# Latent attention with keys on partitions and split products, first two stages fused, on a hybrid decoder layer

## The reference, cut to what matters

```python
xn = rms_norm(x, g_pre)
qa, ka, va, za, cq, ckv_raw, kpe_raw, zb, ma, mb = _split_in(xn @ w_in)
oa = _combine_groups(outs, lses)        # three dilated groups, merged by softmax weights
q = (rms_norm(cq, g_q) @ w_uq)          # 8 heads of 64 + 32 (rotary)
c_kv = rms_norm(ckv_raw, g_kv); k_pe = rope(kpe_raw)
k_nope = c_kv @ w_uk;  v = c_kv @ w_uv  # 64 wide, per head
s = (q_nope . k_nope + q_pe . k_pe) * MLA_SCALE      # 2048 x 2048, causal
ob = softmax(s) @ v
pa = (oa * silu(za)) @ w_proj_a;  pb = (ob * silu(zb)) @ w_proj_b
y = x + rms_norm((sigmoid(ma) * pa + sigmoid(mb) * pb) @ w_out, g_post)
```

## Time and profile before

| | |
|---|---|
| median of 3 executions | 4331.28 us (4324.72 to 4336.58) |
| profiled execution, its span | 4348.47 us, 4346.9 us |
| busy in the span: PE, DVE, ACT, POOL | 3522.2, 1369.5, 951.2, 373.6 us |
| norm and latent stages | 0 to 194.4 us of the span |
| dilated stage | 194.4 to 1536 us |
| gates | 1536 to 2094.8 us |
| latent attention | 2094.8 to 2866 us |
| samples (both stages) | 2866 to 3750 us |
| join | 3750 to 3919 us |
| projection, output | 3919 to 4346.9 us |

### The profile page before, as it was taken

How to read it: one execution, slowest core, us unless ns; L and a number is a source line. 1 busy time by engine, 2 the same in 40 slices (tenths; PEclk the granted TensorE clock), 3 DMA queues, 4 the chain that set the end, 5 groups by cost and what they waited for, 6 DMA issues and landing times. The chain is left out here.

```text
span 4346.9 us, 56892 instructions
## 1 busy us (share of the span) xinstructions
PE 3522.2 (81%) x19368; PEld 2973.9 (68%) x19368; DVE 1369.5 (32%) x3898; ACT 951.2 (22%) x1842; POOL 373.6 (9%) x490
## 2 busy tenths in 40 slices
PE   4899999999999999999799999934444465417989
PEld 3777777777777789999577767723334465317967
DVE  4112222222322321000355556512221222484333
ACT  4322222222222211111244344410000111001021
POOL 0000000000000000000000000002322333002300
PEclk6999999999999889999899999965555777558999
DMA  3243333222333122211200000035552222465543
GB/s 106 89 147 106 106 105 102 88 84 83 95 105 122 56 68 73 74 67 55 66 12 12 14 11 12 10 101 188 185 177 80 61 53 63 141 227 184 175 127 121
DMA packets 310894, 407.39 MB, mean 94 GB/s; under 512 B 72793, under 2 KB 270138, under 8 KB 305290
## 3 DMA queue, kind: packets, MB, share of 16 engines
q1 hardware_dynamic: 278154, 249.11, 19.0%
q0 software_dynamic: 23312, 151.28, 10.0%
q10 hardware_dynamic: 9216, 4.20, 0.3%
HBM read 317.28 MB, written 175.28 MB: 113 GB/s over the span
## 5 line engine op out<-in xcount | busy, mean ns | idle before, releaser
L109 PE MATMUL dil_J<-all_xT_hi,dil_w_hi 128*128 128x512 f32 x1152 | 475.0, 412 | 18.5 <-DVE dil_w_lo L695 17.7
L111 PE MATMUL dil_J<-all_xT_hi,dil_w_lo 128*128 128x512 f32 x1152 | 455.8, 396 | 0.0
L110 PE MATMUL dil_J<-all_xT_lo,dil_w_hi 128*128 128x512 f32 x1152 | 455.5, 395 | 0.0
L109 PE MATMUL gate_ps<-all_xT_hi,gate_w_hi 128*128 128x416 f32 x960 | 338.8, 353 | 9.1 <-DVE gate_w_lo L950 9.1
L110 PE MATMUL gate_ps<-all_xT_lo,gate_w_hi 128*128 128x416 f32 x960 | 337.3, 351 | 0.0
L111 PE MATMUL gate_ps<-all_xT_hi,gate_w_lo 128*128 128x416 f32 x960 | 337.1, 351 | 0.0
L1232 PE MATMUL mla_S<-mla_k,mla_q 96*128 96x512 f32 (+3 forms) x640 | 281.8, 557 | 15.4 <-ACT mla_p L1119 8.7
L720 DVE CUSTOM_DVE_ANT_0 dil_sm<-dil_S,dil_bias 128x256 f32<-128x256 f32 (+1 forms) x384 | 125.0, 363 | 501.2 <-PE dil_S L812 428.7
L109 PEld LDWEIGHTS dil_J<-all_xT_hi,dil_w_hi 128*128 128x128 f32 x1152 | 218.4, 190 | 72.5 <-DVE dil_w_lo L695 17.8
L1260 PE MATMUL mla_O<-mla_v,mla_pT 128*128 128x66 f32 x2176 | 264.8, 271 | 2.6 <-DVE mla_pT L1179 1.7
L666 ACT ACTIVATE dil_sm<-dil_sm,dil_neg 128x256 f32<-128x256 f32 (+1 forms) x384 | 156.6, 455 | 486.6 <-DVE dil_neg L726 486.6
(11 more groups left out here) (264 smaller groups left out, 6102.9 us busy)
## 6 DMA issues: line engine op xcount, KB each, us to landing
out_win_sample<-in_state_win POOLq DMA_DIRECT2D x8, 8128.0 KB, 27.0
sdil_kv<-in_state_win SPq DMA_DIRECT2D x72, 512.0 KB
scr_gates<-gate_out POOLq DMA_DIRECT2D x24, 1040.0 KB, 4.6
sdil_qb<-scr_hs SPq DMA_DIRECT2D x32, 768.0 KB
dil_raw<-in_w_in SPq DMA_DIRECT2D x36, 512.0 KB, 4.1
proj_gm<-scr_gates SPq DMA_DIRECT2D x40, 416.0 KB, 3.3
out_win_sample<-in_state_win POOLq DMA_DIRECT2D x8, 1984.0 KB, 11.5
scr_oa<-dil_rec SPq DMA_DIRECT2D x192, 66.0 KB, 1.6
```

Of the source, the lines that this page charges most:

```text
L109: pe.matmul(out, w[0], x[0], start=first, stop=False)
L110: pe.matmul(out, w[0], x[1], start=False, stop=False)
L111: return pe.matmul(out, w[1], x[0], start=False, stop=last)
```

## The change

**First stages.** stage_norm and stage_latents become stage_front, one pipeline of 22 slots: slot i turns tile i, projects tile i-2 and turns the latents of tile i-4. The weights are loaded by POOL's queue from the start. The copy of the projection to SBUF (L327) is dropped, g_q is applied as a row, the latents' transposes leave in 2 copies instead of 4, and cqT, ckvT, kpeT are stored after every fourth tile.

**Latent attention.** Keys lie on partitions: a unit is now a tile of 128 keys by up to 512 queries, 40 units ("ticks") per head. A first product (A, one fp32r matmul) gives scores with queries on partitions, only to take row maxima; they are put as row 96 of the high queries, so that the transposed scores S come out with the maximum subtracted. S and the output O are split products. ACT writes the exponential and its high part, POOL the remainder. v is laid beside 64 columns of ones, so O holds output and sums, each over 64 partitions. At the end of each of 4 chunks of 512 queries DVE inverts the sums, multiplies by the gate and by O, and the result goes straight to uT. The next head's queries, keys, values (J) and its maxima (A) are made inside the ticks of the current one.

**Join.** The MLA half is gone: no ob, 4 transposes, a gate of 128x512, 4 of 8 blocks of uT.

```diff
+        PROJECT, STATS, TURN, STORE = 2, 3, 4, 5
...
+                def body(i):
+                    if i < TILES:
+                        turn(i)
+                    if 0 <= i - TURN < TILES:
+                        turn_latents(i - TURN)
+                    if 0 <= i - PROJECT < TILES:
+                        project(i - PROJECT)
...
+            @block.gpsimd
+            def _(pool):
+                for c in range(KC):
+                    waits(pool, w_lo, c - 1)
+                    pool.dma_start(raw[c % 2][:, :], t["w_in"][c * P:(c + 1) * P, C_CQ:C_CQ + LAT])\
+                        .then_inc(w_in[c % 2], 16)
...
+        UNITS = [(c, j, max(0, j - 4 * c) * P) for c in range(4) for j in range(4 * c + 4)]
...
+        LAG = 3
+        TICKS = H * NU + LAG
...
+        J_TICKS = (0, 1, 2, 3, 4, 5, 6, 7, 8, 10, 14, 18, 22)
+        SIDE = {tick: [] for tick in range(-1, TICKS)}
+        SIDE[-1] += j_tasks(0)
+        for i, task in enumerate(a_tasks(0)):
+            SIDE[-1 if i < 17 else (i - 17) // 3].append(task)
+        for h in range(1, H):
+            for i, task in enumerate(j_tasks(h)):
+                SIDE[(h - 1) * NU + J_TICKS[i]].append(task)
+            every = a_tasks(h)
+            for i, task in enumerate(every):
+                SIDE[(h - 1) * NU + (NU - 1 if i == len(every) - 1 else 10 + i * 28 // len(every))].append(task)
...
+                    pool.tensor_tensor(pl[b][:, q0:512], p[:, b, q0:512], ph[b][:, q0:512].bitcast(F32),
+                                       ALU.subtract).then_inc(p_lo, 1)
...
+                    act.activation(p[:, n % RING, q0:512], S[n % 2][:, q0:512], ACT.Exp, scale=B_SCALE)\
+                        .then_inc(exped, 1)
...
+                    act.activation(ph[n % RING][:, q0:512], p[:, n % RING, q0:512], ACT.Copy).then_inc(p_hi, 1)
...
+                    dve.reciprocal(inv[r, :], O[b][sums, :]).then_inc(inverted, 1)
+                    dve.wait_ge(inverted, n + 1)
+                    dve.wait_ge(gz_in[b], 16 * (n // 2 + 1))
+                    dve.tensor_tensor(inv[r, :], inv[r, :], gz[b][r, :], ALU.mult).then_inc(gated, 1)
+                    dve.wait_ge(gated, n + 1)
+                    waits(dve, u_stored[b], 16 * (n // 2))
+                    dve.tensor_tensor(u[b][r, :], O[b][r, :], inv[r, :], ALU.mult).then_inc(o_out, 1)
...
+                    waits(pe, a_out, n - 1)
+                    pe.matmul(A[n % 2][:, 0:width], q[h % 2][0][0:NOPE + ROPE, i * P:(i + 1) * P],
...
+                    pe.matmul(out, kh[0:W + 1, rows], qh[0:W + 1, cols], start=True, stop=False)
+                    pe.matmul(out, kh[0:W, rows], ql[0:W, cols], start=False, stop=False)
+                    last = pe.matmul(out, kl[0:W, rows], qh[0:W, cols], start=False, stop=j < 4 * c)
...
+                    pe.matmul(O[o][:, q0:512], vh, ph[b][:, q0:512], start=j == 0, stop=False)
+                    pe.matmul(O[o][:, q0:512], vl, ph[b][:, q0:512], start=False, stop=False)
+                    pe.matmul(O[o][:, q0:512], vh, pl[b][:, q0:512], start=False, stop=end).then_inc(pv_ready, 1)
...
-                    sp.dma_start(ob[b][:, 0:chunks, :, :], t["ob"][rows, 0:chunks]).then_inc(oin[b], 16)
...
-                    for c in range(8):
-                        last = pe.transpose(tp[b][:, c, :], nat[b][:, c // 4, (c % 4) * P:(c % 4 + 1) * P], ident[:, :])
+                    for c in range(4):
+                        last = pe.transpose(tp[b][:, c, :], nat[b][:, c * P:(c + 1) * P], ident[:, :])
```

More of the change, by code:

```diff
@@ L125, in held, with stage_front @@
         eng.sem_inc(ticks, 1)
[L128 to L135, removed]
+def stage_front(nc, t, xT, xs, ident):
     with ExitStack() as ctx:
-        m = Mem(nc, ctx, "norm")
+        m = Mem(nc, ctx, "front")
         xin = [m.sb(f"xin{b}", [P, D]) for b in range(2)]
         xn = [m.sb(f"xn{b}", [P, D]) for b in range(2)]
-        junk = m.sb("junk", [P, D])
         g = m.sb("g_rows", [P, D])
@@ L164, in _ @@
[L164 to L191, removed]
@@ L283, in _, with store_nat @@
                 sp.dma_start(cs[0:NS, NT, :, :], t["rope_rows"][SEQ:TOK]).then_inc(consts, 16)
[L284 to L285 removed]
+                def store_nat(i):
+                    b, r = i % 2, slice(0, rows_of(i))
                     sp.wait_ge(nat_ready, i + 1)
@@ L1272, in _, with free_j, queries @@
-                each_head(pe, body)
+                def free_j(n):
+                    waits(pe, j_act, n - 1)
+                    waits(pe, j_dve, n - 1)
+                def queries(task):
+                    _, h, i = task
+                    n = J_AT[task]
+                    free_j(n)
+                    for c in range(QL // P):
+                        last = pe.matmul(J[n % 2][:, 0:QW], wq[:, c, h, :], cqT[:, c, i * QW:(i + 1) * QW],
+                                         start=c == 0, stop=c == QL // P - 1)
+                    last.then_inc(j_ready, 1)
@@ L1941, in body @@
[L1941 to L1947 removed]
+                    dve.wait_ge(oin[b], (i - b) * 8 + 16)
@@ new lines, in body @@
+                    then(dve.tensor_tensor(top, maxima[0], maxima[1], ALU.max))
+                    then(dve.tensor_tensor(top, top, maxima[2], ALU.max))
+                    for g in range(NG):
+                        last = dve.tensor_tensor(w3[g], maxima[g], top, ALU.subtract)
+                    last.then_inc(expin, 1)
+                    dve.wait_ge(exped, i + 1)
+                    for g in range(NG):
+                        last = dve.tensor_tensor(s3[g], w3[g], sums_of[g], ALU.mult)
@@ new lines, in body @@
+                    then(last)
+                    then(dve.tensor_reduce(sums[:, :], sl[:, :].rearrange("p (g h) -> p h g", h=H), AX.X, ALU.add))
+                    then(dve.reciprocal(sums[:, :], sums[:, :]))
+                    for g in range(NG):
+                        last = dve.tensor_tensor(w3[g], w3[g], heads(sums[:, :]), ALU.mult)
+                    then(last)
+                    wide = wt[:, :].unsqueeze(2).to_broadcast([P, NG * H, HD])
+                    then(dve.tensor_tensor(big[:, :, :].rearrange("p (c s) d -> p c s d", s=2), o,
+                                           wide.rearrange("p (c s) d -> p c s d", s=2), ALU.mult))
```

1062 lines of the change are left out of this document (590 added, 472 removed).

## The result

The changed kernel takes 4346.05 us (median of 12 executions) against 4334.59 for the kernel before, a ratio of 1.0024 (95% interval 1.0014 to 1.0033): no gain, and outside the range that was forecast. One execution of the kernel before took 8954 us, and the ratio leaves it out. One stage ate what two others gave.

What follows compares the result with a forecast made beforehand. TensorE was taken to bound latent attention, no engine being full in the first stages. Gains of 55 (first stages), 16 (latent attention) and 40 (join) sum to 111 us, giving a median of 4220 us, own range 4170 to 4260, wider 4110 to 4300.

Steps and rivals of the forecast that it cites:

- The front: First stages: TensorE paces 17 slots of 5.8 us from about 31 us; 138 to 140 us, a gain of 55.
- The join: Join stage: 16 tiles at 6.9 us, paced by the load of oa, plus 17: 127 us, a gain of 40.
- Latent attention: Attention stage: 755 us where it was 771.2, a gain of 16, with 670 to 840 kept as range.
- the start: Latent attention's opening: loads, then 13 pieces (17 us of VectorE), 17 maxima (12) and key remainder (4): 51 us.
- head 0: Latent attention's first head: carries 27 of its own maxima in ticks 0 to 8, so 105 us.
- heads 1 to 6: Latent attention: 90 us each, from 73.5 of TensorE matmuls, 11.7 lost to stops and 5.1 to half clock.
- The outputs: Latent attention, VectorE: reciprocal 3.3 us, 4.7 per output, four a head; stops of 3.75 at ticks 14 and 26, 4.2 earlier.
- the sentence that found ScalarE's work "hidden": Latent attention: ScalarE's exponentials and copies, 34 x 1.4 = 48 us a head, called hidden under the 90 us head.
- The value pieces: Latent attention: values made on TensorE, 3.6 us every second head, entered as 1.8 a head; VectorE value remainders 1.4.
- The rivals: VectorE never stops TensorE, 4106 us (0.22); slower reciprocal or longer half clock, 4290 (0.18); half clock throughout, 4650 (0.03).
- rival (b): Latent attention: reciprocal of 12 us or more is the bound; gains used up at 866 us; total 4395; chance 0.07.
- the list of signs of being wrong: Reciprocals far from 3.3 us; TensorE waiting for ScalarE or GpSimd instead of VectorE; front slots well above 5.8.

Runs made afterwards that it cites:

- e4: The kernel before with only its two first stages replaced by the fused stage_front: 4274.74 us, ratio 0.9879 to the kernel before.
- e5: The kernel of e1 with the outputs' reciprocal replaced by a copy of the same 512 columns: 4198.79 us, ratio 0.9675 to the kernel before.
- e1: The changed kernel with ScalarE's piece copies moved ahead of the exponential in each tick: 4307.64 us, ratio 0.9957 to the kernel before.
- e7: The kernel of e1 without first products in the three ticks behind the outputs at ticks 14 and 26, more in others: 4233.96 us.
- e6: The kernel of e1 with the first product's causal mask added by TensorE matmuls instead of VectorE: 4304.0 us, ratio 0.9926 to the kernel before.
- e9: The kernel of e7 with query and key pieces moved from behind the outputs at ticks 2 and 6, first products from tick 12: 4280.05 us.
- e8: The kernel of e1 with 14 unused matmuls of 512 columns in TensorE's stream at tick 28 of heads 0 to 6: 4280.62 us.

## Why the prediction was wrong

*The front: right.* The first projection stood at 30.40 us where it was 94.25 (31 forecast), slots at 5.88 (5.8), the next stage's first load at 137.77 (138 to 140). The gain was 57 in the windows, 56 by e4.

```profile
30.40 0.69 PE L107 MATMUL front_pj<-front_w_hi,all_xT_hi 128*128 128x416 f32 x1
```

*The join: the right mechanism, a gain too small.* Of 15 steps from gate to gate 13 took 6.23 to 7.07 us (6.4 to 7 forecast), one 12.66, with VectorE waiting 6.35 for a load of oa, and the last 1.01. The stage took 119 us, not 127: the term was 40, it measured 50. The step was set at 6.9; the mean of the 13 is 6.5.

```profile
3849.36 0.69 DVE L2178 TENSOR_TENSOR join_uT<-join_tp,join_gz 128x512 f32<-128x512 f32 x1 [0.34 <-DVE join_nat L2167]
3855.60 0.69 DVE L2178 TENSOR_TENSOR join_uT<-join_tp,join_gz 128x512 f32<-128x512 f32 x1 [0.26 <-DVE join_nat L2167]
```

*Latent attention: the step that failed.* Forecast 755 us, measured 892, 137 over. By its terms: the start 73 against 51, head 0 129 against 105, heads 1 to 6 624 against 540, the last head, its tail and the stage's end 66 against 59.

The outputs were not the error. A reciprocal of 3.36 us, stops of 3.9 and 3.7 behind the outputs and of 4.3 at tick 4, and a VectorE sum of 66.9 us a head (67 forecast) are all as worked out. Behind the 3.73 us stop the clock was a mean of 0.62 for 4.5 us. The rule of the Trainium skill, "TensorE: Matmul & The Clock Gate", section "HAM oscillation — how this bites in real kernels", that the price of a cold clock comes again with each such gap, is borne out by these stops. Not every gap has it: one of 1.71 us, at tick 4 of head 2 in e5, left the clock at 1.00. What the Trainium skill says of the reciprocal ("VectorE: DVE Perf Modes", section "First, the fixed hardware budget") led to an estimate of 4.3 us; the trace has 3.36, and the measurement decides.

What failed is the sentence that found ScalarE's work "hidden": it compared sums of busy time, 48 us a head, and did not follow the order in ScalarE's stream. The value pieces were entered at TensorE's matmuls alone, 3.6 us in each of three heads (1.8 as a mean). They cost 17 (112.5 against 95.5): 9.4 more of idle TensorE, 3.6 of matmuls, the rest half clock. So 13.4 us in each of these heads were not forecast, 40 of the 84 us over in heads 1 to 6, and e1 gives back 10.3 a head by order alone.

The other 44 us are 7.3 in each of the six heads, and of these most is a mis-sized sum. A head without value pieces was to take 88.2 us, of which 71.7 for matmuls; it took 95.5. By e5, its matmuls alone take 77.0: the six score and value matmuls of a tick, each counted to its end or to the start of the next, sum to 53.0 us there over the head, where 48.0 were entered at 0.235 for 512 columns. Idle time was 13.2 us instead of 11.7 (head 2), and half clock added 5.6 instead of 5.1 (82.6 busy against 77.0).

The start failed likewise. The first matmul came where it was forecast, at 2048.6, 18.6 us into the stage; then the split of the rotary keys took 10 us (4 forecast), the 13 pieces 25 (17) and the 17 maxima 20 (12). Each had been worked out from VectorE alone. VectorE's work in the three was 37 us where 33 were forecast, so some 17 of the 22 us over are waiting. The split shows how: ScalarE's high part of the rotary keys stands behind a copy of the causal mask, whose load landed only at 2052.0, and VectorE's remainder waits for that high part.

```profile
2052.03 0.31 ACT L1217 ACTIVATE mla_causalr<-mla_causal 128x128 fp32r<-128x128 f32 x1 [9.21 <-DMA mla_causal<-in_causal]
2052.37 3.70 ACT L1220 ACTIVATE mla_k_hi<-mla_p 32x2048 fp32r<-32x2048 f32 x2
2054.38 4.49 DVE L1309 TENSOR_TENSOR mla_k_lo<-mla_p,mla_k_hi 32x2048 fp32r<-32x2048 f32 x2 [5.93 <-ACT mla_k_hi L1220]
```

Pieces go from TensorE to ScalarE, VectorE and back through two banks, at a mean granted clock of 0.66. No experiment touched the start. Head 0 makes 27 more maxima in its first ticks; e1 gave it back 10.7 of 24 us, and what holds the rest was not tried.

*The rivals.* Latent attention passed the point of rival (b), 866 us, by a mechanism none of the rivals had; the total came out near no change only because front and join gave 107 us against the 121 that attention lost. A rival with a chain through three in-order engines was missing; the list of signs of being wrong had TensorE waiting for ScalarE, and the trace has it at one remove, TensorE for VectorE and VectorE for ScalarE. Another order recovers 112 us (e7 against the changed kernel) without any instruction removed, so the loss was one of order more than of work. Of these, 38 (e1) are waits that the forecast had at nothing; the other 74 are for the most part the stops at the outputs, which it had counted as part of the price.

## What to carry to other kernels

Where several engines pass pieces to each other and each has a fixed order, sums of busy time per engine are a lower bound only: follow one piece through every stream and write down what stands ahead of it there, above all work of a different chain. Spread the work of the second busiest engine by place: behind each long piece of it (here an output of 4.9 us), leave ticks without other work on it. Moving work away from two places gained 74 us (e7); taking VectorE's masks away at all places, for small matmuls on TensorE, gained nothing that could be told (e6). Follow the new order by the same rule: e9 emptied two more places and lost 46 us, in part because the pieces it moved now waited for each other on ScalarE.

## What the hardware showed that was not expected

The clock's price of a pause was not one figure: behind the same stop of 3.73 us, TensorE was at half clock for 3.3 us in the changed kernel and for 6.7 in e1, and filling it with idle matmuls (e8) took 2.3 us off the tick behind it, more work on TensorE included. Cutting a VectorE chain of three instructions of 512 columns into four of 128 made it 2 us longer (8 us for four outputs). The product of the inverse and the gate, with both operands in SBUF, took a mean of 898 ns where the one with an operand in PSUM took 688:

```profile
L1384 DVE TENSOR_TENSOR mla_inv<-mla_inv,mla_gz 64x512 f32<-64x512 f32 x31 | 27.8, 898 | 1.1
...
L1387 DVE TENSOR_TENSOR mla_u<-mla_O,mla_inv 64x512 f32<-64x512 f32 x31 | 21.3, 688 | 1.1
```

GpSimd is at work on SBUF in the same ticks. That this is the cause shows best at another VectorE instruction with both operands in SBUF, the sum of a rotated query piece (L1326): beside an idle GpSimd it took 582 or 583 ns, 17 times; seven times it took 1397 to 1492, each begun within 0.06 us after an instruction of GpSimd. One of the seven:

```profile
2065.85 1.05 POOL L1179 TENSOR_TENSOR mla_q_lo<-mla_turned,mla_q_hi 32x416 fp32r<-32x416 f32 x1 [3.34 <-ACT mla_q_hi L1240]
```

```profile
2065.86 1.49 DVE L1326 TENSOR_TENSOR mla_turned<-mla_turned 32x416 f32<-32x416 f32 x1
```
